# A second cycle of both MLPs computed by Strassen's scheme, in a two-layer fp32 transformer step

## The chip, the cores and the metric

The kernel runs on one core of one Trainium2 chip. The metric is the device time in microseconds (us) of one execution, as the median of a few runs. The four compute engines are TensorE (PE, with its weight loads as PEld), VectorE (DVE), ScalarE (ACT) and GpSimd (POOL); SyncE (SP) issues nearly all DMAs. They run side by side and meet at semaphores.

## The reference, cut to what matters

The reference is one step of a hybrid backbone with two layers on 640 tokens (512 latent, 128 context) of width 1024. Layer 0 mixes by a convolution module and a retention scan, layer 1 by grouped-query attention. The change touches only the MLP that ends each layer:

```python
h = rmsnorm(x, norm_g[layer, 1]) * (1 + sc2) + sh2
x = x + g2 * (jnp.square(jax.nn.relu(h @ mlp_w1[layer])) @ mlp_w2[layer])
```

with `mlp_w1` of 1024x4096 and `mlp_w2` of 4096x1024. The scales, shifts and gates (`sc2`, `sh2`, `g2`) come from the conditioning vector times `ada_w`, a product that in layer 0 is computed in small pieces between the matmuls of the MLP, for what follows it.

## The kernel before

**Number format.** Each fp32 operand is split into a high part (what fp32r keeps, a copy by ScalarE) and a low part (operand minus high part, by VectorE or GpSimd). A product is three matmuls: high by high, high by low, low by high. Names end in H and L (`hH`, `hL`; `wH`, `wL`; `fH`, `fL`). Tokens stand in the free dimension as two halves of 320 columns, so that nearly each matmul is 128x128 weights by 320 columns.

**The MLP by cycles.** `CYCLES` = 8 cycles of 512 hidden columns run one behind the other. A cycle has a first product (h times 1024x512 of `mlp_w1`), relu and square, and a second product (the square times 512x1024 of `mlp_w2`) that is added into `xT`. The first `PLAIN` = 2 cycles are plain: 8 x 4 x 2 x 3 = 192 matmuls for each product, 384 a cycle. Cycles 2 to 6 (the set `W2`) use one level of Strassen's scheme (Winograd's form) in both products: seven half-size products instead of eight, so 7 x 24 = 168 matmuls for each, 336 a cycle. The last cycle has the first product by Strassen and the second plain.

**What a Strassen product needs.** The weights' seven operands are B11, B22, B21, read from HBM, and four sums, T1 = B12 - B11, T3 = B22 - B12, T2 = T3 + B11, T4 = B21 - T2 (`add_blocks`; the keys are "p" for the first product, "q" for the second). VectorE makes the sums, ScalarE the high parts (`split_product`), and the low parts are made by VectorE for T2, T3, T1, B22, B21, T4 of "p" (`P_DVE`, made by `t_lo`) and by GpSimd for B11 of "p" and all of "q" (`lo`, L2033). High and low parts lie in a ring of four buffers (`wH`, `wL`), the raw blocks in another ring of four, and SyncE loads a block when the buffer's last reader has signalled (`wait_raw_free`). The tokens' side of the first product needs A11, A12, A22, which are views of h, and four sums S1 to S4 of blocks of h. These are the same in all cycles, so they are made once a layer (`add_s` L2511, `s_split` L1830, `s_low` L2525), before the change in cycles 0 and 1. The high and low part of S1 take the place of the block of h in `hH` and `hL` that only plain cycles read.

**Order inside a first Strassen product.** TensorE goes B11, T2, T3, T1, B22, B21, T4, two groups (m = 0, 1) of 12 matmuls each. B11, T2, T3, T4 accumulate in banks 6 and 7; between them ScalarE copies the partial sums out (`partials` L1764: `p1` after B11, `u2` after T2, `u3` after T3), and T2's first group waits for `p1`. B22's groups accumulate on T1's banks once VectorE has taken T1's sum out (`combine` L2582), which waits in VectorE's program order behind two weight sums, "p" T4 and "q" T3. "q" T3 needs the raw block "q" B22 from HBM. At the end of a Strassen cycle ScalarE splits B11, T2, T3 and T1 of the next one, in this order, and only then turns to `p1`; VectorE makes the sums T3, T2, T1, the low parts of T2 and T3 and the updates `product_out` (L2617, L2620, L2622) in a written order.

**Layer 0 alone** also has three short products with `ada_w` in each cycle (`strips`, L866; in a Strassen cycle the first stands between B11 and T2, the second between T1 and B22, the third between T4 and T1 of the second product), the 1 MB loads of `ada_w` for them in SyncE's queue between the weight blocks, and `modulate` on VectorE.

**The plain cycle.** ScalarE takes the relu out of the bank (L1758), VectorE squares it (L2500), ScalarE and VectorE split the square; then 16 groups of the second product run through four banks, each bank free when VectorE's `residual` (L2069) of the group four places before is done. VectorE's further work (`s_steps`, `p_add`, `t_lo`) is written out by group number (`after`).

Of the kernel before, what the change touches and what calls it, by code (L numbers as in the profile page):

```python
# [26 lines left out]
P = 128  # L27
# [4 lines left out]
HALF = T // 2  # L32
# [13 lines left out]
CYCLES = FF // 512  # L46
PLAIN = 2
# [40 lines left out]
P_DVE, SUM_ORDER = (T2, T3, T1, B22, B21, T4), (T3, T2, T1, T4)  # L88
# [56 lines left out]
F_CYCLE = {0: 0, 1: 8, CYCLES - 1: 16}  # L145
F_LAYER = 24
# [106 lines left out]
def hybrid_step(nc, x_prompt, x_sample, state_ret, cache_k, cache_v, ada_w, even_w_in, even_w_out, final_g,  # L253
# [3 lines left out]
    with ctx:  # L257
# [3 lines left out]
        def place(name, shape, dt=F32):  # L261
# [77 lines left out]
        s4_raw = nc.alloc_sbuf_tensor_at("s4_raw", [P, 4, HALF], F32, offset=here[0] + 24 * HALF)  # L339
# [5 lines left out]
        s1_raw = nc.alloc_sbuf_tensor_at("s1_raw", [P, 4, HALF], F32, offset=here[0])  # L345
# [392 lines left out]
        def _(pe):  # L738
# [436 lines left out]
            def first_strassen(layer, c, v, part):  # L1175
# [13 lines left out]
                pe.wait_ge(s_ready, 4 * layer + 4)  # L1189
# [262 lines left out]
        def _(act):  # L1452
# [291 lines left out]
            def mlp_layer(layer):  # L1744
# [102 lines left out]
                for c in range(CYCLES):  # L1847
                    t, g, s = t0 + 4 * c, g0 + G_CYCLE[c], WINO * layer + c - PLAIN
                    if 0 < c < PLAIN:
# [5 lines left out]
                        s_split(2, 5)  # L1855
                        s_split(3, 6)
                        s_split(4, 8)
                    elif c:
                        partials(c, p1, 1, p1_done)
                        split_product("p", s, B22, g + 2)  # L1860
                        partials(c, u2, 3, u2_done)
                        split_product("p", s, B21, g + 4)
                        partials(c, u3, 5, u3_done)
                        split_product("p", s, T4, g + 6)
                    if c in W2:
# [19 lines left out]
                        for n, i in enumerate((B11, T2, T3, T1)):  # L1885
                            split_product("p", s + 1, i, g + 30 + 4 * n)
# [173 lines left out]
        def _(dve):  # L2060
# [71 lines left out]
            def h_both(norm, later):  # L2132
# [10 lines left out]
                h_lo(norm, 0, KC - 1)  # L2143
                reciprocal_std(norm, 1)
# [333 lines left out]
            def mlp_layer(layer, norm):  # L2478
# [37 lines left out]
                r2, r3, r4 = (s_raw[i][:] for i in (2, 3, 4))  # L2516
                s_steps = [lambda: add_s(r3, *h_block(0, 1), ALU.add), lambda: add_s(r2, *h_block(4, 1), ALU.add),
                           lambda: add_s(s1_raw[:], r3, r2, ALU.add, 2), lambda: add_s(r4, *h_block(0, 0), ALU.add),
                           lambda: add_s(r2, s1_raw[:], r4, ALU.subtract, 4), lambda: add_s(r3, r4, r3, ALU.subtract, 4),
                           lambda: add_s(r4, *h_block(4, 0), ALU.add, 6), lambda: add_s(r4, r4, r2, ALU.subtract, 7)]  # L2520
# [112 lines left out]
                def strassen_cycle(c):  # L2633

                    s, s2 = WINO * layer + c - PLAIN, len(W2) * layer + c - PLAIN
                    t_lo(s, T1)
                    modulate(c, 0)
# [48 lines left out]
                    t_lo(s + 1, T2)  # L2686
# [3 lines left out]
                    t_lo(s + 1, T3)  # L2690
# [38 lines left out]
                for c in range(CYCLES):  # L2729
                    if c == 0:  # L2730
                        hidden(0, {5: [lambda: weight_lo(t0 + 2)]})
                    elif c < PLAIN:
                        hidden(c, {2: [lambda: modulate(c, 0)], 3: s_steps[4:5], 4: s_steps[5:6], 5: s_steps[6:7],
                                   6: s_steps[7:8]})
# [6 lines left out]
                    if c == 0:  # L2741
                        modulate(0, 1)
                    after = {8: [lambda: modulate(c, 2)]} if c % 2 == 0 else {10: [lambda: modulate(c, 2)]}
                    if c == 0:
                        after.update({2 + 2 * n: after.get(2 + 2 * n, []) + [step] for n, step in enumerate(s_steps[:4])})
                    if c == PLAIN - 1:
                        for n, i in ((8, T3), (9, T2), (11, T1)):
                            after[n] = after.get(n, []) + [lambda i=i: p_add(WINO * layer, i)]
                        for n, i in ((12, T2), (14, T3)):
                            after[n] = after.get(n, []) + [lambda i=i: t_lo(WINO * layer, i)]  # L2750
                        after[1] = [lambda: s_low(2, 1)]
                        after[3] = [lambda: s_low(3, 2)]
                        after[4] = [lambda: s_low(4, 3)]
                        after[5] = [lambda: s_low(1, 4)]
# [216 lines left out]
```

## Time and profile before

| | us |
|---|---|
| median of 3 runs | 1544.29 (1543.58 to 1544.55) |
| the profiled execution's own time | 1546.61 |
| its span, first to last instruction | 1544.8 |
| PE busy in it | 1513.4 (98%) |
| DVE busy | 1157.0 (75%) |
| ACT busy | 682.6 (44%) |
| POOL busy | 550.1 (36%) |
| mean granted TensorE clock | 0.996 of full speed |

Shares are of the span. A matmul's record is longer than the spacing of matmuls, because they are pipelined; so the time of many matmuls is read from starts, or from a stretch. The MLP of layer 0 runs from about 415 to 863 us, that of layer 1 from about 1108 to 1530 us; cycle 1 of them starts at 478.1 and 1166.7.

### The profile page before, as it was taken

How to read it: one execution, taken by the hardware profiler on the slowest of the kernel's cores; microseconds unless marked ns; L12 is line 12 of the kernel's file. 1: busy time of each engine (PE TensorE's matmuls, PEld its weight loads, DVE VectorE, ACT ScalarE, POOL GpSimd, SP SyncE). 2: the span in 40 equal slices, each digit the busy share in tenths (PEclk: the TensorE clock that was granted, in tenths of full speed). 3: DMA queues.
4: the chain of work that ended last, by engine and by line, in shares of the span. 5: the costliest groups of instructions: out<-in, count | busy, mean ns of one | idle time of the engine just before them, and what ended most of it. 6: DMA issues, size and time to landing. Idle time of an engine off the chain costs nothing. (4 is left out here: it accounts for less than half of the span.)

```text
span 1544.8 us, 28343 instructions
## 1 busy us (share of the span) xinstructions
PE 1513.4 (98%) x11754; PEld 1476.9 (96%) x11754; DVE 1157.0 (75%) x1901; ACT 682.6 (44%) x1140; POOL 550.1 (36%) x362
## 2 busy tenths in 40 slices
PE   8999999999999999999999999999999999999998
PEld 7999999999999999999999999999999999999998
DVE  5348678675684878898897888773584798899886
ACT  5323333334442354455455534652442355545553
POOL 0233313314323343563454253101333265446531
PEclk9999999999999999999999999999999999999999
DMA  9455334213233334433435121001222222322222
GB/s 327 154 177 168 102 101 154 83 53 125 76 123 109 124 118 165 134 135 132 137 131 169 35 83 62 28 1 55 83 69 69 69 69 81 98 82 69 83 83 83
DMA packets 123168, 162.20 MB, mean 105 GB/s; under 512 B 4640, under 2 KB 87584, under 8 KB 123040
## 3 DMA queue, kind: packets, MB, share of 16 engines
q1 hardware_dynamic: 121808, 159.34, 32.0%
q8 instruction: 93, 1.52, 0.4%
q10 hardware_dynamic: 1232, 1.05, 0.2%
q14 instruction: 35, 0.29, 0.1%
HBM read 156.44 MB, written 3.93 MB: 104 GB/s over the span
## 5 line engine op out<-in xcount | busy, mean ns | idle before, releaser
L2033 POOL TENSOR_TENSOR wL<-raw,wH 128x512 fp32r<-128x512 f32 x188 | 304.8, 1648 | 793.6 <-ACT wH L1463 532.0
L1171 PE MATMUL ps<-fx,wH 128*128 128x320 f32 x1120 | 248.0, 310 | 1.6 <-DVE held L2622 1.1
L747 PE MATMUL ps<-hH,wH 128*128 128x320 f32 x704 | 221.1, 314 | 1.9 <-DVE hL L2119 1.3
L747 PE MATMUL ps<-hH,wL 128*128 128x320 f32 x704 | 217.6, 309 | 0.0
L747 PE MATMUL ps<-hL,wH 128*128 128x320 f32 x704 | 217.5, 309 | 0.0
L1171 PEld LDWEIGHTS ps<-fx,wH 128*128 128x128 f32 x1120 | 186.8, 188 | 4.6 <-issue 4.0
L2033 POOL TENSOR_TENSOR wL<-raw_high,wH 128x512 fp32r<-128x512 f32 x100 | 141.1, 1438 | 128.2 <-ACT wH L1463 114.1
L1171 PE MATMUL ps<-fx,wL 128*128 128x320 f32 x560 | 173.0, 309 | 0.0
L747 PE MATMUL ps<-wH,hH 128*128 128x256 f32 x560 | 162.1, 290 | 2.4 <-POOL wL L2033 1.1
L747 PE MATMUL ps<-wL,hH 128*128 128x256 f32 x560 | 158.3, 283 | 0.0
L747 PE MATMUL ps<-wH,hL 128*128 128x256 f32 x560 | 158.3, 283 | 0.0
L2069 DVE SCALAR_TENSOR_TENSOR xT<-ps,modT,xT 128x192 f32<-128x192 f32 (+1 forms) x216 | 86.1, 433 | 79.5 <-PE ps L747 78.7
L747 PEld LDWEIGHTS ps<-hH,wH 128*128 128x128 f32 x704 | 132.2, 188 | 6.4 <-DVE hL L2119 2.8
L1171 PE MATMUL ps<-s,wH 128*128 128x320 f32 x576 | 128.9, 312 | 7.8 <-ACT p L1764 6.3
L747 PEld LDWEIGHTS ps<-hL,wH 128*128 128x128 f32 x704 | 132.2, 188 | 0.2
L747 PEld LDWEIGHTS ps<-hH,wL 128*128 128x128 f32 x704 | 132.2, 188 | 0.0
L747 PE MATMUL ps<-fH,wH 128*128 128x320 f32 x384 | 119.8, 312 | 0.2 <-DVE fL L2491 0.2
L1171 PE MATMUL ps<-hL,wH 128*128 128x320 f32 x384 | 118.7, 309 | 0.0
L1171 PE MATMUL ps<-hH,wL 128*128 128x320 f32 x384 | 118.6, 309 | 0.0
L1171 PE MATMUL ps<-hH,wH 128*128 128x320 f32 x384 | 118.6, 309 | 0.0
L747 PE MATMUL ps<-fL,wH 128*128 128x320 f32 x384 | 118.6, 309 | 0.0
L747 PE MATMUL ps<-fH,wL 128*128 128x320 f32 x384 | 118.6, 309 | 0.0
(303 smaller groups left out, 3753.7 us busy)
## 6 DMA issues: line engine op xcount, KB each, us to landing
ada<-in_ada_w SPq DMA_DIRECT2D x40, 1024.0 KB, 5.7
raw<-in_mlp_w SPq DMA_DIRECT2D x64, 512.0 KB, 3.8
raw_high<-in_mlp_w SPq DMA_DIRECT2D x64, 512.0 KB, 3.8
raw<-in_even_w_in SPq DMA_DIRECT2D x28, 512.0 KB, 5.8
pre_w<-in_ada_w SPq DMA_DIRECT2D x16, 512.0 KB, 8.9
raw<-in_odd_w_qkv SPq DMA_DIRECT2D x10, 512.0 KB, 3.6
raw<-in_even_w_out SPq DMA_DIRECT2D x8, 512.0 KB, 3.7
raw<-in_odd_w_o SPq DMA_DIRECT2D x6, 512.0 KB, 3.5
```

The lines of the kernel that those rows point to most:

```text
L747: last = nc.tensor.matmul(ps[:, bank, 0:width], a_, b_, start=(k == 0 and p_ == 0), stop=(k == nk - 1 and p_ == 2))
L1171: last = nc.tensor.matmul(ps[:, bank, 0:HALF], a_, b_, start=(opens and k == 0 and p_ == 0), stop=(k == nk - 1 and p_ == 2), skip_group_ch ...
L2033: last = nc.gpsimd.tensor_tensor(wL[:, at % 4, cs], source(key)[:, cs], wH[:, at % 4, cs].bitcast(F32), ALU.subtract)
L2069: last = nc.vector.scalar_tensor_tensor(out=x, in0=ps[:, n % 4, c0 - half * HALF:c0 - half * HALF + w_], scalar=modT[:, gate_at + k, which ...
```

## The change

`PLAIN` becomes 1, so that cycle 1 of both layers is a Strassen cycle and `W2` is 1 to 6. What was spread over cycles 0 and 1 for the first Strassen cycle now stands in cycle 0. The order of the sums of h changes, the first (of `hH` + `hL`, block 0, half 0) goes into the norm ahead of the MLP, behind the low parts of half 0 (`h_both`), one into the squares (`hidden`), and the others between the updates of the second product. The low part of S4 and that of T1 come at the start of cycle 1. The raw sums get other buffers: S2's over the end of `fq` and `p1`, S3's over `u2` and `u3`, S1's and S4's over the norm buffers and `held`, the first T3 over `fr`. TensorE, and ScalarE's partials, wait for each S by itself and not for all four.

`P_DVE` now differs by layer: in layer 0 the low parts of T2 and T3 of "p" are GpSimd's, in layer 1 VectorE's as before. And in layer 1, ScalarE's split of T1 moves from the end of the cycle before to behind `p1` in the cycle that uses it.

```diff
-PLAIN = 2
+PLAIN = 1
-P_DVE, SUM_ORDER = (T2, T3, T1, B22, B21, T4), (T3, T2, T1, T4)
+SUM_ORDER = (T3, T2, T1, T4)
+P_DVE = ((T1, B22, B21, T4), (T2, T3, T1, B22, B21, T4))
...
+        t3_begin = nc.alloc_sbuf_tensor_at("t3_begin", [P, 1024], F32, offset=here[0])
+        s2_raw = nc.alloc_sbuf_tensor_at("s2_raw", [P, 4, HALF], F32, offset=here[0] + 24 * HALF)
...
                 wait_low(pe, "p", s, T2)
-                pe.wait_ge(s_ready, 4 * layer + 4)
+                pe.wait_ge(s_ready, 4 * layer + 1)
...
                 wait_low(pe, "p", s, T3)
+                pe.wait_ge(s_ready, 4 * layer + 2)
...
                     if out is p1 and c == PLAIN:
-                        act.wait_ge(s_ready, 4 * layer + 4)
+                        act.wait_ge(s_sum, 8 * layer + 8)
+                        act.wait_ge(s_ready, 4 * layer + 1)
+                    elif out is u2 and c == PLAIN:
+                        act.wait_ge(s_ready, 4 * layer + 2)
...
                         partials(c, p1, 1, p1_done)
+                        if layer:
+                            split_product("p", s, T1, g)
                         split_product("p", s, B22, g + 2)
...
-                        for n, i in enumerate((B11, T2, T3, T1)):
+                        for n, i in enumerate((B11, T2, T3) if layer else (B11, T2, T3, T1)):
                             split_product("p", s + 1, i, g + 30 + 4 * n)
...
                     for q in range(4):
+                        if q == 1:
+                            s_split(4, 8)
...
+                        elif q < 3 or layer == 0:
                             split_product("p", s + 1, (B11, T2, T3, T1)[q], g + 8 + 4 * (q + 1))
-                        if c == PLAIN - 1 and q == 0:
+                        if q == 0:
                             act.wait_ge(acc_full, g + 8)
-                            s_split(1, 3)
+                            s_split(1, 4)
+                            s_split(3, 5)
+                            s_split(2, 6)
...
                 h_lo(norm, 0, KC - 1)
+                if norm in (1, 3):
+                    dve.wait_ge(h_ready, 16 * norm + 8)
+                    nc.vector.tensor_tensor(s_raw[2][:], hH[:, 0:4, 0:HALF].bitcast(F32), hL[:, 0:4, 0:HALF].bitcast(F32),
+                                            ALU.add).then_inc(s_sum, 1)
                 reciprocal_std(norm, 1)
...
                     t_lo(s, T1)
+                    if c == PLAIN:
+                        s_low(4, 4)
                     modulate(c, 0)
                     t_lo(s, B22)
...
-                    t_lo(s + 1, T2)
+                    if layer:
+                        t_lo(s + 1, T2)
...
-                    t_lo(s + 1, T3)
+                    if layer:
+                        t_lo(s + 1, T3)
...
+                        hidden(0, {5: [lambda: weight_lo(t0 + 2)], 6: s_steps[0:1]})
...
+                    after = {0: s_steps[1:2], 2: s_steps[2:3], 3: s_steps[3:4], 5: s_steps[4:5], 6: s_steps[5:6],
+                             8: [lambda: modulate(0, 2)] + s_steps[6:7], 9: [lambda: s_low(2, 3)],
+                             10: [lambda: p_add(p0, T3)], 11: [lambda: p_add(p0, T2)], 12: [lambda: s_low(3, 2)],
+                             13: [lambda: p_add(p0, T1)], 14: [lambda: t_lo(p0, T2)] if layer else [],
+                             15: ([lambda: t_lo(p0, T3)] if layer else []) + [lambda: s_low(1, 1)]}
```

## Rows read from the trace of the kernel before

**Rows 1.** The page: busy us of an engine, its share of the span, instructions.
```profile
PE 1513.4 (98%) x11754; PEld 1476.9 (96%) x11754; DVE 1157.0 (75%) x1901; ACT 682.6 (44%) x1140; POOL 550.1 (36%) x362
```
**Rows 2.** Waits of PE, whole span: us in total, times, longest.
```profile
PE ps L1171 <- ACT p L1764: 6.3, 5, 1.3
```
**Rows 3.** Stretches, by the cycles of both MLPs: length, busy us of each engine, granted clock.
```profile
478.10:538.20 60.10, 60.10 (x482) 58.69 (x481) 39.39 (x57) 19.07 (x28) 20.53 (x12) 1.00 0.33 106
538.20:591.20 53.00, 53.00 (x434) 51.81 (x433) 42.09 (x59) 25.98 (x35) 23.64 (x16) 1.00 0.39 130
591.20:645.90 54.70, 53.34 (x434) 51.73 (x433) 46.29 (x64) 26.95 (x36) 26.75 (x16) 1.00 0.41 136
645.90:699.40 53.50, 53.12 (x434) 51.72 (x433) 47.79 (x61) 26.99 (x36) 25.20 (x16) 1.00 0.40 138
...
1166.70:1223.30 56.60, 56.60 (x386) 56.36 (x385) 38.62 (x53) 19.06 (x28) 20.56 (x12) 1.00 0.19 57
1223.30:1273.00 49.70, 49.60 (x339) 49.36 (x338) 41.77 (x54) 25.04 (x34) 26.86 (x16) 1.00 0.25 75
1273.00:1324.10 51.10, 49.72 (x338) 49.25 (x337) 46.32 (x60) 26.64 (x36) 26.83 (x16) 1.00 0.27 83
```
**Rows 4.** Timeline of PE, start of layer 1's cycle 3: start, us, instruction [idle before].
```profile
1276.18 0.31 PE L1171 MATMUL ps<-hL,wH 128*128 128x320 f32 x1
1276.32 0.31 PE L1171 MATMUL ps<-hH,wL 128*128 128x320 f32 x1
1277.91 0.53 PE L1171 MATMUL ps<-s,wH 128*128 128x320 f32 x2 [1.28 <-ACT p L1764]
```
**Rows 5.** Timeline of ACT, the same place.
```profile
1276.38 1.06 ACT L1481 ACTIVATE wH<-raw 128x1024 fp32r<-128x1024 f32 x1 [1.54 <-DVE raw L2566]
1277.35 0.75 ACT L1764 ACTIVATE p<-ps 128x320 f32<-128x320 f32 x2
```
**Rows 6.** Timeline of DVE, the same cycle.
```profile
1279.67 1.22 DVE L2531 TENSOR_TENSOR wL<-raw_high,wH 128x1024 fp32r<-128x1024 f32 x1
1285.74 1.23 DVE L2566 TENSOR_TENSOR t_first<-raw_high,raw 128x1024 f32<-128x1024 f32 x1
```
**Rows 7.** Load of "q" B22 in that cycle: first and last issue; then time to landing.
```profile
L541 SPq DMA_DIRECT2D raw_high<-in_mlp_w x1: 367/367/367, 1280.9 to 1280.9; - x1
...
DMA to landing us min/median/max: 4.5/4.5/4.5
```
**Rows 8.** Timeline of DVE, layer 0's cycle 3.
```profile
607.14 1.23 DVE L2566 TENSOR_TENSOR t_first<-raw_high,raw 128x1024 f32<-128x1024 f32 x1 [3.58 <-DMA raw_high<-in_mlp_w]
608.29 0.48 DVE L2582 TENSOR_TENSOR fq<-ps,u 128x320 f32<-128x320 f32 x1
```
**Rows 9.** Timeline of PE, layer 0's cycle 3.
```profile
608.92 0.53 PE L1171 MATMUL ps<-s,wH 128*128 128x320 f32 x2 [1.24 <-DVE fq L2582]
```
**Rows 10.** Timeline of DVE, layer 1, norm and cycle 0.
```profile
1117.05 2.16 DVE L2098 RECIPROCAL ps<-rstd 128x320 f32<-128x320 f32 x1 [2.59 <-ACT rstd L1494]
...
1144.68 2.33 DVE L2511 TENSOR_TENSOR s_raw<-hH,hL 128x1280 f32<-128x1280 f32 x1
1146.93 1.20 DVE L2069 SCALAR_TENSOR_TENSOR xT<-ps,modT,xT 128x192 f32<-128x192 f32 x3
...
1151.69 1.48 DVE L2511 TENSOR_TENSOR s_raw<-s_raw 128x1280 f32<-128x1280 f32 x1
```
**Rows 11.** Timeline of POOL, the low parts: two instructions make one block.
```profile
581.31 2.56 POOL L2033 TENSOR_TENSOR wL<-raw_high,wH 128x512 fp32r<-128x512 f32 x2 [0.71 <-ACT wH L1481]
...
607.84 3.89 POOL L2033 TENSOR_TENSOR wL<-raw,wH 128x512 fp32r<-128x512 f32 x2 [20.87 <-ACT wH L1481]
```
**Rows 12.** Timeline of POOL: the slowest pair of layer 1.
```profile
1203.52 5.04 POOL L2033 TENSOR_TENSOR wL<-raw,wH 128x512 fp32r<-128x512 f32 x2
```
**Rows 13.** Timeline of ACT, end of layer 0's cycle 2.
```profile
590.08 1.06 ACT L1481 ACTIVATE wH<-t_first 128x1024 fp32r<-128x1024 f32 x1 [7.26 <-DVE t_first L2566]
591.04 1.05 ACT L1481 ACTIVATE wH<-t_second 128x1024 fp32r<-128x1024 f32 x1
```

More of the change, by code:

```diff
@@ L120, with T_LOW_AT @@
     raw_last_[buf_] = key_
+def T_LOW_AT(s, i):
+    layer, n = divmod(s, WINO)
+    return layer * WINO * len(P_DVE[0]) + n * len(P_DVE[layer]) + P_DVE[layer].index(i) + 1
 BLOCK_AT = {key: n for n, key in enumerate(BLOCKS)}
-POOL_LO = [key for key in BLOCKS if key[0] == "q" or (key[2] not in P_DVE if key[0] == "p" else key[0] not in DVE_LO)]
+POOL_LO = [key for key in BLOCKS if key[0] == "q" or (key[2] not in P_DVE[key[1] // WINO] if key[0] == "p" else key[0] not in DVE_LO)]
 POOL_AT = {key: n + 1 for n, key in enumerate(POOL_LO)}
@@ L144 @@
 A_MLP1 = A_QKV + 30
-F_CYCLE = {0: 0, 1: 8, CYCLES - 1: 16}
-F_LAYER = 24
+F_CYCLE = {0: 0, CYCLES - 1: 8 * PLAIN}
+F_LAYER = 8 * PLAIN + 8
 def F_AT(c, half, k):
@@ L338, in hybrid_step @@
         fs = nc.alloc_sbuf_tensor_at("fs", [P, 2, HALF], F32, offset=here[0] + 16 * HALF)
-        s4_raw = nc.alloc_sbuf_tensor_at("s4_raw", [P, 4, HALF], F32, offset=here[0] + 24 * HALF)
+        t3_begin = nc.alloc_sbuf_tensor_at("t3_begin", [P, 1024], F32, offset=here[0])
+        s2_raw = nc.alloc_sbuf_tensor_at("s2_raw", [P, 4, HALF], F32, offset=here[0] + 24 * HALF)
         fq = place("fq", [P, 4, 2, HALF])
@@ L344, in hybrid_step @@
         p1 = place("p1", [P, 2, HALF])
-        s1_raw = nc.alloc_sbuf_tensor_at("s1_raw", [P, 4, HALF], F32, offset=here[0])
+        s3_raw = nc.alloc_sbuf_tensor_at("s3_raw", [P, 4, HALF], F32, offset=here[0])
         u2 = place("u2", [P, 2, HALF])
@@ L350, in hybrid_step @@
         t24_first = place("t24_first", [P, 1024])
-        s2_raw, s3_raw = (nc.alloc_sbuf_tensor_at(f"s{n}_raw", [P, 4, HALF], F32, offset=norm_buffers + 16 * HALF * j)
-                          for j, n in enumerate((2, 3)))
+        s1_raw, s4_raw = (nc.alloc_sbuf_tensor_at(f"s{n}_raw", [P, 4, HALF], F32, offset=norm_buffers + 16 * HALF * j)
+                          for j, n in enumerate((1, 4)))
         s_raw = {1: s1_raw, 2: s2_raw, 3: s3_raw, 4: s4_raw}
-        t3_begin = nc.alloc_sbuf_tensor_at("t3_begin", [P, 1024], F32, offset=norm_buffers)
         held = nc.alloc_sbuf_tensor_at("held", [P, KC, HALF], F32, offset=norm_buffers)
@@ L504, in wait_low @@
         def wait_low(engine, *key):
-            if key[0] == "p" and key[2] in P_DVE:
-                engine.wait_ge(t_low, len(P_DVE) * key[1] + P_DVE.index(key[2]) + 1)
+            if key[0] == "p" and key[2] in P_DVE[key[1] // WINO]:
+                engine.wait_ge(t_low, T_LOW_AT(*key[1:]))
             elif key in FIRST_BLOCKS:
@@ L1197, in first_strassen @@
                 wait_low(pe, "p", s, T1)
+                pe.wait_ge(s_ready, 4 * layer + 3)
                 pe.wait_ge(dve_free, v)
@@ L1202, in first_strassen @@
                 wait_low(pe, "p", s, B22)
+                pe.wait_ge(s_ready, 4 * layer + 4)
                 for m in range(2):
@@ L2514, in h_block @@
                     return [x[:, k0:k0 + 4, halfcols(half)].bitcast(F32) for x in (hH, hL)]
[L2516 to L2520, printed above, removed]
+                r1, r2, r3, r4 = (s_raw[i][:] for i in (1, 2, 3, 4))
+                s_steps = [lambda: add_s(r4, *h_block(0, 1), ALU.add), lambda: add_s(r1, *h_block(4, 1), ALU.add),
+                           lambda: add_s(r1, r4, r1, ALU.add, 3), lambda: add_s(r3, r2, r4, ALU.subtract, 3),
+                           lambda: add_s(r2, r1, r2, ALU.subtract, 5), lambda: add_s(r4, *h_block(4, 0), ALU.add, 5),
+                           lambda: add_s(r4, r4, r2, ALU.subtract, 7)]
                 def s_low(i, count):
@@ L2730, in mlp_layer @@
                     if c == 0:
[L2731 to L2734, printed above, removed]
+                        hidden(0, {5: [lambda: weight_lo(t0 + 2)], 6: s_steps[0:1]})
                     elif c in W2:
@@ L2740, in mlp_layer @@
                         break
[L2741 to L2754, printed above, removed]
+                    modulate(0, 1)
+                    p0 = WINO * layer
+                    after = {0: s_steps[1:2], 2: s_steps[2:3], 3: s_steps[3:4], 5: s_steps[4:5], 6: s_steps[5:6],
[3 more added lines that the diff above has]
+                             15: ([lambda: t_lo(p0, T3)] if layer else []) + [lambda: s_low(1, 1)]}
                     for n in range(16):
```

4 lines of the change are left out of this document (removed).

## The prediction, made before the changed kernel was run

> **What bounds the kernel now.** I read the page's busy times first [rows 1]: TensorE is busy 98% of the span, no other engine over 75%. So what counts is how many matmuls there are, and the little time that TensorE waits. Second, TensorE's waits [rows 2]: the largest group by far is five waits for ScalarE's copy `p1`, 6.3 us together. Third, the stretches cut at the cycles [rows 3]. The granted clock is 1.00 in all of them. A plain cycle takes 60.1 us in layer 0 and 56.6 in layer 1; the first Strassen cycle 53.0 and 49.7; a later one 54.7 or 53.5 and 51.1. The ratio 56.6 / 384 gives 0.147 us a matmul, and 336 of them make 49.4, so the first Strassen cycle of layer 1 has almost no idle time. Layer 0's 53.0 holds 3.6 more for three short products, 1.2 each. Two things are to be seen: the later cycles are 0.5 to 1.7 us longer than the first, and in them VectorE is busy 46 to 48 us of 51 to 54, near a bound of its own.
>
> Fourth, the timelines at the place of a wait. In layer 1 the last matmul of B11 starts at 1276.32 and the first of T2 at 1277.91 where 1276.47 was due [rows 4]: 1.44 us lost. ScalarE shows why [rows 5]: it could have copied `p1` soon after 1276.4, but its split of T1 stands ahead, and that began only at 1276.38, when VectorE had made the sum. The wait comes in cycles 3 to 7, five times. Layer 0 hides it behind its short product. There another wait shows: at 607.14 VectorE has sat idle 3.58 us for a block from HBM [rows 8], and TensorE starts B22 at 608.92, 1.24 idle [rows 9], 0.63 behind the start of the combination at 608.29.
>
> **The change part by part.** The sum is made on the profiled execution, 1546.6 us, of which 1544.8 is the span; the median of the runs is 1544.3, 2.3 less, and the saving is carried over to it.
>
> *Matmuls.* Each converted cycle loses 48, so 96 x 0.147 = 14.1 us go. By the stretches: cycle 1 falls from 56.6 to 49.7 in layer 1 and from 60.1 to 53.0 in layer 0 if the new first Strassen cycle is as clean as the old one. That is -6.9 and -7.1; the short products stay three.
>
> *T1 split behind `p1`, layer 1.* `p1` is then ready with B11's end. Behind it the split of T1 ends about 1278.3, before VectorE comes to T1's low part at 1278.5 (it ends where the next row begins, 1279.67 [rows 6]), so nothing there moves. `u2` waits behind the splits of T1 and B22 (1.06 each) and is ready some 0.3 before T3 wants it. So 1.44 goes, five times, and one later cycle more exists. What is late next: the load of "q" B22 is issued when VectorE has done B22's low part, 1280.9, and takes 4.5 [rows 7]. It lands at 1285.4, just ahead of the sum at 1285.74 [rows 6]. This does not move, while TensorE comes 1.44 earlier. The sum then ends at 1286.6, B22 can start 0.63 behind that, 1287.3; due are six groups behind T2, 1276.47 + 72 x 0.147 = 1287.1. So 0.2 comes back, and a later cycle of layer 1 takes 51.1 - 1.44 + 0.2 = 49.9. Bounds: 49.5 (nothing back) to 51.1 (all back). I take the lower part, since each step has a row.
>
> *Norm.* The new sum of h (1.4 to 1.5 us) stands where VectorE idles 2.59 us for the standard deviation [rows 10]; in both layers, so nothing.
>
> *Cycle 0.* VectorE had room; now it makes all sums of h and three weight sums there. From the first update, at 1143.2 in layer 1: 16 updates at 0.46 (half 0) and 0.66 (half 1, two instructions; three instructions took 1.2 [rows 10]) are 9.0; six sums of h at 1.45 are 8.7, three low parts of them 4.3, three weight sums 3.4, low parts of T2 and T3 2.3; together 27.7. A sum that met GpSimd took 2.33 and not 1.48 [rows 10], and GpSimd has four instructions in the first part; I add 2. VectorE is through at about 1173, 6 us into cycle 1, and its updates stay ahead of the banks by 0.5 to 3 us, except near group 8 where I put 0.3 us of waiting (bounds 0 and 1.5). T2's low part comes at 1169.6, due 1170.3: in time. But T1's and S4's low parts follow (1.15 + 1.4), then B22's at 1176.6, 9.9 us into the cycle. The load of "q" B22 starts there, 3.8 us at that quiet time (the 4.5 of rows 7 overlaps another), the sum takes 1.2, B22 can start at +15.5, due 96 x 0.147 = +14.1: about 1.3 us of waiting. Bounds: 0 (VectorE's own slack is taken) and 3.
>
> *Layer 0, cycle 1.* The same with one `modulate` more, GpSimd working on T2 and T3 against VectorE's last low parts, and a 1 MB load in the queue ahead of "q" B22. I come to B22's low part at +11, landing at +16.4, B22 at +18.2, due +14.1 and two short products, +16.5: 1.7 to 2, taken as 2.0 (bounds 0 and 4; the nearest row, cycle 3, lost 1.7 in the same wait).
>
> *T2 and T3 low parts to GpSimd, layer 0.* Their high parts are ready at 591.1 and 592.1 [rows 13]; GpSimd is idle from 587 to 607.8 [rows 11] and takes 2.56 for a block, 3.9 when it meets VectorE. T2 is due at 591.2 + 3.5 + 1.2 = 595.9 and comes at 593.7 to 595.0; T3 due 599.4, comes at 596.3 to 598.9. So it is hidden, with 0.5 us to spare at the worst. VectorE loses 2.3 us of work just where it is late: T1's and B22's low parts come 1 us earlier, hence the load behind the 3.58 us gap [rows 8] too. I give cycle 3 a gain of 1.0, cycles 4 to 6 of 0.25 each, and cycle 2, now a later one, costs 0.2. Bounds for the part: a gain of 3.2 (all that cycles 3 to 6 have over 53.0 [rows 3]) and a loss of 3.
> The Trainium skill (SBUF — State Buffer, "Who interferes with whom") says that a VectorE instruction with two SBUF inputs and a GpSimd instruction reading SBUF exclude each other for a whole instruction, whoever starts first. The trace agrees with its 2.33 against 1.48; by it four more GpSimd instructions could hold VectorE up to four times a cycle, which would eat the gain and bring this part to about 0.
>
> *Sum.* Layer 0: cycle 1 -60.1 + 53.0 + 2.0 = -5.1; cycle 2 +0.2; cycle 3 -1.0; cycles 4 to 6 -0.75: -6.65. Layer 1: cycle 0 +0.3; cycle 1 -56.6 + 49.7 + 1.3 = -5.6; cycle 2, 49.7 to 49.9, +0.2; cycles 3 to 6 and the first product of 7, -1.2 each, -6.0: -11.1. Together -17.8: 1546.6 - 17.8 = 1528.8 for a profiled execution, and a median of 1526.5.
>
> **The rivals.**
> *B, the gain of the moved split is given back.* For it: VectorE has only some 4.8 us idle in a later cycle of layer 1 (46.3 of 51.1 [rows 3]), and the load's time does not move. Against: its idle time lies before the place where it becomes late. If all five waits return (+6.2), or the first Strassen cycles wait 3 us more each, the time is 1532.7.
> *C, all is hidden.* No waits in cycle 1 of either layer (-3.3), none in cycle 0 and none returned (-1.5), layer 0's later cycles at 53.0 (-1.7): 1520.0. Against it: the load of "q" B22 hangs on a late VectorE in both layers.
> *D, GpSimd is late for T3 (slower than before).* In layer 0 the two blocks of low parts come in each of cycles 1 to 7. If their four instructions go at the slowest pair's pace (5.04 for a block [rows 12]) and each block waits once more for a VectorE instruction, T3 is ready at 591.1 + 10.1 + 2.3 = 603.5, 4.1 us late; 7 x 4.1 = 29 us, so 1555. It decides against the change from 2.5 us a cycle on (17.8 / 7). Against it: the pace of rows 11, and GpSimd's 20 us of idle time at that place.
> *E, the low parts are on the path once each.* GpSimd takes 2.56 where VectorE takes 1.22 for the same block; 14 blocks x 1.35 = 19 us, all of it on the path, gives 1545.5, no change.
> The Trainium skill (GPSIMD Engine Reference, "Engine selection") says to put elementwise work on VectorE because GpSimd is about twice as slow with two inputs; this is E. The trace agrees with the ratio (2.56 to 1.22), but shows slack ahead of T2 and T3.
>
> **How the numbers follow.** Forecast 0.57, with its own range 1522.5 to 1530.5; B 0.20; C 0.15; E 0.04; D 0.04. A change under 0.2% (3.1 us) can't be told from none here; only E falls within it and only D is slower, so faster 0.92, same 0.04, slower 0.04. The range goes from below C to above B, 1519 to 1534, and leaves out E, D and the ends of B and C, near 0.15.
>
> **What would show it.** Right: 96 matmul records fewer; the group "PE ps <- ACT p" gone from TensorE's waits; later cycles of layer 1 near 49.9 with a small wait for `fq` at B22; cycle 1 near 51.0 and 55.0 with its wait at B22 behind the HBM block; GpSimd busy some 3 us more in each cycle of layer 0. Wrong: a wait of TensorE for `wL` of GpSimd at T2 or T3 (D, E); later cycles of layer 1 near 51 with the wait at B22, or at T2 of the second product (B); cycle 0 longer than 0.5 us more.

## The result

| | median us | runs | range us | ratio to before, 95% |
|---|---|---|---|---|
| before | 1544.25 | 4 | 1543.58 to 1544.55 | |
| changed | 1531.28 | 4 | 1529.75 to 1531.53 | 0.9911 [0.9899, 0.9923] |

The change takes 13.0 us away. The forecast was 1526.5 (range 1519 to 1534, own range of the likeliest case 1522.5 to 1530.5): the sign and the range held, the saving is 13.0 instead of 17.8, and the number lies nearer to rival B's 1532.7. The profiled execution of the changed kernel took 1531.19 us with a span of 1529.3.

The page after, line by line beside [rows 1]: 96 matmuls fewer, VectorE busy 51.6 us more (the sums and low parts of a second converted cycle in each layer), GpSimd 53.9 more.

```profile
PE 1499.2 (98%) x11658; PEld 1462.3 (96%) x11658; DVE 1208.6 (79%) x1925; ACT 708.8 (46%) x1162; POOL 604.0 (39%) x390
```

TensorE's waits in the whole span, beside [rows 2]: three groups of the changed kernel (us in total, times, longest). The group for ScalarE's `p`, 6.3 us, is gone. What has grown is VectorE's `fq` (B22 of the first product), 1.2 us before, `held` (T2 of the second product), 1.1 before, and the last low parts `fL` of cycle 0's squares, 0.2 before.

```profile
PE ps L1180 <- DVE fq L2604: 2.9, 5, 0.8
PE ps L1180 <- DVE held L2644: 2.8, 7, 0.6
PE ps L756 <- DVE fL L2513: 2.6, 3, 1.0
```

The stretches by cycles, beside [rows 3]: layer 0's cycles 0, 1, 3 and 6, then layer 1's 0 to 3.

```profile
414.37:478.14 63.77, 61.88 (x484) 59.18 (x483) 60.34 (x102) 29.11 (x54) 20.64 (x15) 1.00 0.36 116
478.14:531.13 52.99, 52.99 (x435) 51.74 (x433) 47.99 (x65) 26.41 (x35) 33.01 (x20) 1.00 0.42 140
584.06:637.02 52.96, 52.96 (x434) 51.76 (x433) 44.31 (x62) 26.68 (x36) 31.68 (x20) 1.00 0.41 140
743.50:798.31 54.81, 53.47 (x435) 51.75 (x433) 47.42 (x61) 27.06 (x36) 33.14 (x20) 1.00 0.40 135
1088.86:1160.41 71.55, 69.60 (x467) 68.33 (x465) 66.11 (x115) 34.25 (x61) 20.94 (x14) 1.00 0.20 60
1160.41:1210.88 50.47, 49.77 (x339) 49.31 (x337) 47.03 (x58) 24.92 (x34) 27.20 (x16) 1.00 0.28 84
1210.88:1261.15 50.27, 49.76 (x338) 49.29 (x337) 46.98 (x60) 26.77 (x36) 27.25 (x16) 1.00 0.28 84
1261.15:1311.43 50.28, 49.67 (x339) 49.29 (x337) 47.19 (x60) 26.77 (x36) 27.43 (x16) 1.00 0.28 85
```

Cut in the same way in the kernel before, layer 0's cycle 0 took 62.63 and layer 1's 69.71. The converted cycle 1 is as short as hoped or shorter (52.99, 50.47). Layer 1's later cycles are 50.3, where 49.9 was forecast. Layer 1's cycle 4 is the exception, 50.58. And both cycles 0 are longer, by 1.14 and 1.84 us, where 0 and 0.3 were forecast.

### The profile page after: what moved, and what is told of

The parts are those of the page before. It is cut to its first block and busy times, and to the rows that moved or that the text cites. A ratio compares the mean times of both kernels' runs of the same rounds, so it can differ in the third digit from the quotient of the medians.

```text
span 1529.3 us, 28267 instructions
## 1 busy us (share of the span) xinstructions
PE 1499.2 (98%) x11658; PEld 1462.3 (96%) x11658; DVE 1208.6 (79%) x1925; ACT 708.8 (46%) x1162; POOL 604.0 (39%) x390
## 5 line engine op out<-in xcount | busy, mean ns | idle before, releaser
L1180 PE MATMUL ps<-fx,wH 128*128 128x320 f32 x1344 | 297.5, 310 | 3.0 <-DVE held L2644 2.8
L1180 PEld LDWEIGHTS ps<-fx,wH 128*128 128x128 f32 x1344 | 224.1, 188 | 6.2 <-issue 5.9
L1180 PE MATMUL ps<-fx,wL 128*128 128x320 f32 x672 | 207.6, 309 | 0.0
L1180 PEld LDWEIGHTS ps<-fx,wL 128*128 128x128 f32 x672 | 126.2, 188 | 0.0
L2051 POOL TENSOR_TENSOR wL<-t_second,wH 128x512 fp32r<-128x512 f32 x60 | 101.7, 1716 | 52.9 <-ACT wH L1493 52.7
L1180 PEld LDWEIGHTS ps<-s,wH 128*128 128x128 f32 x672 | 111.5, 188 | 7.8 <-issue 6.0
L756 PEld LDWEIGHTS ps<-hH,wH 128*128 128x128 f32 x576 | 108.2, 188 | 6.0 <-DVE hL L2137 2.8
L756 PEld LDWEIGHTS ps<-wH,hH 128*128 128x128 f32 x560 | 107.2, 191 | 3.6 <-DVE xT L2087 1.4
L2087 DVE SCALAR_TENSOR_TENSOR xT<-ps,modT,xT 128x320 f32<-128x320 f32 (+2 forms) x168 | 66.8, 432 | 55.4 <-PE ps L756 55.1
L756 PEld LDWEIGHTS ps<-hL,wH 128*128 128x128 f32 x576 | 108.2, 188 | 0.2
```

The costliest lines, as they stand in the source:

```text
L756: last = nc.tensor.matmul(ps[:, bank, 0:width], a_, b_, start=(k == 0 and p_ == 0), stop=(k == nk - 1 and p_ == 2))
L1180: last = nc.tensor.matmul(ps[:, bank, 0:HALF], a_, b_, start=(opens and k == 0 and p_ == 0), stop=(k == nk - 1 and p_ == 2), skip_group_ch ...
L2051: last = nc.gpsimd.tensor_tensor(wL[:, at % 4, cs], source(key)[:, cs], wH[:, at % 4, cs].bitcast(F32), ALU.subtract)
L2087: last = nc.vector.scalar_tensor_tensor(out=x, in0=ps[:, n % 4, c0 - half * HALF:c0 - half * HALF + w_], scalar=modT[:, gate_at + k, which ...
```

## Where the two terms went wrong, in the trace

*Cycle 0.* VectorE, GpSimd and TensorE in layer 1, where the square's last two groups are made (start, us, instruction, idle before):

```profile
1130.97 1.49 DVE L2533 TENSOR_TENSOR s_raw<-hH,hL 128x1280 f32<-128x1280 f32 x1
1132.37 1.59 DVE L2522 TENSOR_TENSOR fs<-fr 128x320 f32<-128x320 f32 x1
1133.88 3.04 DVE L2513 TENSOR_TENSOR fL<-fs,fH 128x320 fp32r<-128x320 f32 x2
```
```profile
1132.19 5.88 POOL L2051 TENSOR_TENSOR wL<-raw_high,wH 128x512 fp32r<-128x512 f32 x4 [25.24 <-ACT wH L1475]
```
```profile
1136.98 0.41 PE L756 MATMUL ps<-fH,wH 128*128 128x320 f32 x1 [0.78 <-DVE fL L2513]
```

The sum of h moved into the squares (1130.97) pushes the square of group 7 to 1132.37, just behind GpSimd's first low part. From there the two engines alternate: each of three VectorE instructions of 0.49 us takes 1.5 to 1.6, the length of a GpSimd instruction. TensorE's third group of the second product waits twice, 1.79 us together, in layer 1 and once, 0.78, in layer 0.

The kernel before had a little of this. In its layer 1 only the last low part met GpSimd, behind a wait for ScalarE's copy, which stood behind the split of a weight tile; TensorE waited 0.22:

```profile
1141.62 1.64 DVE L2491 TENSOR_TENSOR fL<-fs,fH 128x320 fp32r<-128x320 f32 x1 [1.41 <-ACT fH L1752]
```

*Later cycles of layer 1.* VectorE's chain in cycle 3, from the first sum of the second product's weights to the first product group:

```profile
1273.53 1.23 DVE L2588 TENSOR_TENSOR t_first<-raw_high,raw 128x1024 f32<-128x1024 f32 x1 [1.25 <-DMA raw_high<-in_mlp_w]
1274.68 0.49 DVE L2604 TENSOR_TENSOR fq<-ps,u 128x320 f32<-128x320 f32 x1
...
1276.61 2.33 DVE L2553 TENSOR_TENSOR wL<-raw_high,wH 128x1024 fp32r<-128x1024 f32 x1
1278.87 0.48 DVE L2604 TENSOR_TENSOR fq<-ps,u 128x320 f32<-128x320 f32 x1
1279.27 1.92 DVE L2588 TENSOR_TENSOR raw<-raw 128x1024 f32<-128x1024 f32 x1
1281.11 0.48 DVE L2604 TENSOR_TENSOR fq<-ps,u 128x320 f32<-128x320 f32 x1
1281.51 1.52 DVE L2630 TENSOR_TENSOR fx<-fq,fx 128x640 fp32r<-128x640 f32 x1
...
1286.64 2.31 DVE L2588 TENSOR_TENSOR t_second<-raw_high,t_second 128x1024 f32<-128x1024 f32 x1
1288.87 0.81 DVE L2630 TENSOR_TENSOR fx<-u,fx 128x640 fp32r<-128x640 f32 x1
1289.61 0.88 DVE L2644 TENSOR_TENSOR held<-ps,held 128x320 f32<-128x320 f32 x2
```
```profile
1290.23 0.39 PE L1180 MATMUL ps<-fx,wH 128*128 128x320 f32 x1 [0.61 <-DVE held L2644]
```

It runs 16.6 us with 0.65 us of idle time. Four of its instructions take longer than usual beside GpSimd (2.33, 2.31 and 1.92 where 1.22 is usual, 1.52 where 0.81 is usual), which works from 1276.57 to 1287.87: 3.6 us. In the kernel before VectorE had caught up with TensorE once on this way, in the second of the two `fq<-ps,p`,

```profile
1295.79 0.49 DVE L2582 TENSOR_TENSOR fq<-ps,p 128x320 f32<-128x320 f32 x1 [0.94 <-PE ps L1171]
```

since TensorE had lost 1.44 us at `p1`. Now it does not. The last matmul ahead of T2 starts at 1289.32, so T2 was due 0.147 later, at 1289.47, and came 0.76 late; with 0.16 late at B22 that is all of the 0.9 us that a later cycle (50.28) takes over its 336 matmuls at 0.147 (49.4). The prediction had 0.2 returned at B22 and left the old 0.35 at T2 as it was, without looking there.

## The experiments

All are edits of the changed kernel. Differences are those of the medians, against the 1531.38 us of its second run; the intervals in brackets are for the ratio to the kernel before and are 4 to 5 us wide, so a difference under 2 us rests on the stretches of the traces, one trace each. Both kernels were traced a second time: the changed kernel unchanged,

> The changed kernel unchanged, a second profile and five more rounds, as the base for its neighbours. Theory S (the sum of h that stands among the squares of cycle 0 makes the lateness there): cycle 0 again 63.8 us in layer 0 and 71.5 in layer 1, with TensorE idle 0.8 and 1.8 us in the third group of the second product. Rival N (that was an accident of one execution): cycle 0 back near 62.6 and 69.7. Time 1530 to 1532 either way.

gave 1531.38 us (1530.97 to 1532.93), ratio 0.9916 [0.9901, 0.9931], a span of 1529.1 and the same cycles 0 to the hundredth, 63.77 and 71.55. So theory S's lateness is no accident. One thing was: layer 0's cycle 6, 54.81 in the first trace, is 53.51 here. The kernel before:

> The kernel before once more, for a second trace: its first profiled execution lay 2.3 us above its median. If that was an accident of one stage, one stretch is some 1 us longer in the first trace than in this one and the span is near 1542.5; if the profile adds it, the span is 1544.8 again.

It took 1543.64 with a span of 1541.8. Of the 3.0 us between the two spans, 0.85 lie in layer 0's cycles 5 and 6, 0.3 ahead of cycle 1, and 1.75 in its cycle 3, 54.72 in the first trace [rows 3, 8, 9] and here

```profile
583.84:636.81 52.97, 52.97 (x434) 51.73 (x433) 46.84 (x61) 27.01 (x35) 26.49 (x17) 1.00 0.42 144
```

So the 1.24 us wait of [rows 9], from which the prediction took a gain, was an accident of that execution. What differs is the load of "q" B22: it landed 8.4 us after its issue in the long cycle 3 and 6.2 in this one, and 8.1 in the 54.81 us of the changed kernel's cycle 6 against 6.9 in its 53.51. Each time the 1 MB load issued just ahead of it was late as well (8.3 and 6.0, 8.7 and 7.5). Why the loads took longer is not shown.

**Cycle 0.** Three edits.

```
# e_sum_n5:    hidden(0, {5: [weight_lo(t0 + 2), s_steps[0]]})      (was 6: s_steps[0:1])
# e_act_order: hidden_hi(0, 7); split(t0 + 3, g0 + 8)               (was the other way round)
# e_sum_after: hidden(0, {5: [weight_lo(t0 + 2)]}); after = {0: s_steps[0:1], 1: s_steps[1:2], ...
```

> The first sum of h in cycle 0 goes ahead of the square of group 6 instead of behind it; the same instructions, the same count. There VectorE idles 1.68 us (layer 0) and 0.48 us (layer 1) for ScalarE. Theory S (the short squares come one behind the other, each held by a GpSimd instruction of 1.5 us): the square of group 7 starts 1.5 and 0.5 us earlier, one of the three held instructions gets ahead of GpSimd's block, cycle 0 loses 1 us in layer 0 and 1.5 in layer 1, total -2.5 us. Rival V (VectorE's work in cycles 0 and 1 together is the bound, wherever it stands): cycle 0 shorter by as much, but B22 of cycle 1 waits 1.5 us more in layer 1; total -1. Rival N: no change.

Measured 1529.72 (1529.19 to 1530.42), 0.9904 [0.9889, 0.9919], 1.7 us less than the changed kernel. In the traces cycle 0 is 62.64 in layer 0 (-1.13) and 1.03 shorter in layer 1: theory S, where -1 and -1.5 were expected. Only one `fL` is held now. Cycle 1 of layer 1 is 50.77, and 50.47 and 50.55 in the two traces of the changed kernel: V takes back 0.3 us at most.

> ScalarE copies the high part of the last square of cycle 0 before it splits the next weight tile, instead of behind it; nothing else changes. GpSimd's four low parts of that tile can start only behind the split, so they no longer meet the last two low parts of the squares. Theory S with contention as its cause: the two instructions that took 1.56 us take 0.49, TensorE's third group of the second product waits 0.5 us or less, cycle 0 is 1.0 us shorter in layer 0 and 1.8 in layer 1, the total falls by 1.5 to 2.8 us. If the sum's own 1.49 us is the cause and not the contention: at most 0.5 us in each layer, total -0.5 to -1. Rival V: gained in cycle 0, given back in cycle 1 of layer 1; total -1.

Measured 1528.31 (1526.95 to 1529.25), 0.9894 [0.9877, 0.991], 3.1 us less. The same place in layer 1, VectorE and then GpSimd:

```profile
1129.49 1.49 DVE L2533 TENSOR_TENSOR s_raw<-hH,hL 128x1280 f32<-128x1280 f32 x1
1130.89 0.49 DVE L2522 TENSOR_TENSOR fs<-fr 128x320 f32<-128x320 f32 x1
1131.29 1.12 DVE L2513 TENSOR_TENSOR fL<-fs,fH 128x320 fp32r<-128x320 f32 x2
```
```profile
1132.91 10.05 POOL L2051 TENSOR_TENSOR wL<-raw_high,wH 128x512 fp32r<-128x512 f32 x4 [27.43 <-ACT wH L1475]
```
```profile
1087.38:1156.61 69.23, 69.08 (x467) 68.32 (x465) 63.64 (x115) 34.25 (x61) 25.20 (x14) 1.00 0.20 62
```

The sum of h stands where it stood and takes as long; the three short instructions behind it take 0.49 each (the two `fL` together 1.12, with a short pause), and TensorE's wait at this place is gone. Cycle 0 is 2.32 us shorter in layer 1, 1.13 in layer 0. That is the contention, and not the sum's own 1.49 us. The swap also lets ScalarE's copy come earlier, but in the changed kernel VectorE had no idle time for that copy (rows above), and ScalarE itself stood idle for 0.93 us until VectorE had made the square. By an estimate from these rows (ScalarE's split over at 1133.06, a copy of 0.47, then 0.49), both `fL` would have been done at about 1134.0 without the contention, and TensorE wanted the first at 1134.33. The contention does not vanish: GpSimd's four instructions take 10.05 now instead of 5.88, but nobody waits for them. In layer 1 the cycle is also 0.48 shorter than in the kernel before (69.23 to 69.71), so part of these 3.1 us is the old lateness of the last `fL` and no loss of the change. Cycle 1 of layer 1 is 50.69, so V takes back 0.2 at most.

> The first sum of h leaves the squares of cycle 0 and stands behind its first update, the next one behind the second. Theory S: the squares of cycle 0 go as in the kernel before, cycle 0 is 62.6 and 69.7 us, -1.1 and -1.8. But all later work of VectorE in the cycle stands where it did while TensorE comes 1.8 us earlier. Rival V (VectorE's chain sets cycle 1 of layer 1): T2's low part of cycle 1 ends at the same time as before, due 1.8 us earlier, and B22 waits 2.3 instead of 0.5; the total is within 0.5 us of the changed kernel in layer 1 and -1.1 in layer 0: -1.1. Without V the total is -2.9.

Measured 1530.88 (1529.93 to 1532.08), 0.9912 [0.9897, 0.9926], 0.5 less, which the intervals don't tell from nothing. In the trace cycle 0 is 63.14 in layer 0 and 0.6 shorter in layer 1, 1.25 us in sum of the 2.9; in part of the rest's stead TensorE waits, here in layer 1:

```profile
PE ps L756 <- DVE xT L2087: 0.7, 2, 0.3
PE ps L756 <- DVE fL L2513: 0.2, 1, 0.2
```

Cycle 1 did not become longer (50.52), so V, whose total was nearer, had the place wrong: what is lost is lost within cycle 0, most of it at the updates. S is right about the cause, wrong in that the sum could simply be put elsewhere.

**The parts undone.**

```
# e_split_back: layer 1: split_product("p", s + 1, T1, ...) again at the end of the cycle before
# e_low_dve:    P_DVE = (T2, T3, T1, B22, B21, T4) for both layers, t_lo of T2, T3 in both
```

> One part undone: in layer 1 ScalarE splits T1 again at the end of the cycle before, ahead of its copies p1. Theory P (the prediction's step: the wait for p1 is worth 1.44 us a cycle, less what returns at B22): the group of TensorE's waits for ScalarE's p comes back, later cycles of layer 1 go from 50.3 to 51.1, cycle 1 stays at 50.5 (its T1 is split late anyway) or gains as well; total +0.8 x 5 to +1.3 x 6, so 1535.5 to 1539. Rival G (the wait is only exchanged for the one at B22 and for VectorE's later lateness): total +1.5 or less.

Measured 1535.57 (1534.99 to 1536.97), 0.9944 [0.9932, 0.9957]: +4.2 us, theory P, at the lower end. Over the whole span, and a later cycle:

```profile
PE ps L1180 <- ACT p L1776: 7.5, 6, 1.2
```
```profile
1213.34:1264.50 51.16, 49.76 (x338) 49.30 (x337) 46.39 (x60) 26.66 (x35) 26.92 (x16) 1.00 0.27 83
```

The wait of [rows 2] is back, six times, and a later cycle takes 51.15, as before. So the split is worth 51.15 - 50.3 = 0.85 us a cycle, not 1.2.

> One part undone: T2's and T3's low parts are VectorE's in layer 0 as well, and GpSimd has 14 blocks less. Theory M (VectorE's load is what made layer 0's later cycles long): cycle 3 back from 53.0 to 54.7, the others within 0.3 of 52.9 to 53.5, cycle 1 from 53.0 to 54.5 with a wait at B22; total +2 to +4 us, 1533.5 to 1535.5. Rival R (it makes no difference in layer 0, which has slack by its short products): within 0.7 us of 1531.4.

Measured 1534.0 (1532.23 to 1535.61), 0.9933 [0.992, 0.9945]: +2.6 us, within M's numbers. But the trace has little of M: layer 0's cycle 1 is 53.20 (not 54.5), cycle 2 53.51 (+0.6), cycle 3 52.99 (not 54.7), cycle 4 0.6 shorter; a cycle 6 of 54.78 and 1 us in layer 1's cycle 4 have appeared in other kernels too. Cycle 6's is a late load of "q" B22 again (8.1 us). I read 0.3 to 0.8 us for the part itself from the stretches; whether the rest of the median's 2.6 is chance or the part's own stays open.

**The later cycles of layer 1.**

```
# e_pool_t3:  P_DVE[1] without T3; GpSimd makes T3's low part in layer 1
# e_t4_after: layer 1: q_add(s2, T4) behind the first four product_out instead of ahead of operand_lo(S2_)
# e_fill_gap: e_act_order, and in layer 1  combine(c, F11, 0); t_lo(s, T4); q_add(T3); combine(c, F11, 1); q_add(T2)
#             (was q_add(T3); combine(c, F11, 0); q_add(T2); combine(c, F11, 1); t_lo(s, T4))
```

> One step further: in layer 1 T3's low part (not T2's) goes to GpSimd. Theory L (a later cycle of layer 1 waits 0.5 us at B22 since VectorE's row of low parts T3, T1, B22 frees B22's buffer late and the load behind it lands at 1324.45 with 1324.5 the sum's start): VectorE is through with B22's low part 0.4 to 0.6 us earlier (the splits of ScalarE come 0.6 ahead of VectorE now), the wait goes nearly, later cycles 49.8, total -2 to -3. Rival X (what VectorE gains in its own work it loses to GpSimd's instructions in the same stretch, each of which holds one of its own): total between -0.7 and +2.

Measured 1533.65 (1532.07 to 1534.48), 0.993 [0.9916, 0.9944]: +2.3, beyond both ranges. Later cycles stay at 50.3, so theory L is out and the rows are rival X's; what X does not hold is the rest, for 1.5 of the 1.6 us that this trace's span is longer lie in layer 1's cycle 0 and have another cause, shown behind the next run. Why VectorE was not earlier, in cycle 3 (VectorE, then GpSimd):

```profile
1263.07 1.22 DVE L2553 TENSOR_TENSOR wL<-t_first,wH 128x1024 fp32r<-128x1024 f32 x1
1264.21 2.31 DVE L2588 TENSOR_TENSOR raw<-raw 128x1024 f32<-128x1024 f32 x1
```
```profile
1264.06 3.62 POOL L2051 TENSOR_TENSOR wL<-t_second,wH 128x512 fp32r<-128x512 f32 x2 [5.20 <-ACT wH L1493]
```

The 1.22 us taken off VectorE come back as 1.1 us on the sum that meets GpSimd. B22's load is issued 7.98 us into the cycle, against 7.94 in the changed kernel.

> Measures the disputed cost: in layer 1 the load of the second product's block B22 brings only half of its rows (0.26 of 0.52 MB), so this kernel leaves out the new values of the other half. Theory L: the load lands 1 us or more earlier, the sum q T3 starts at once behind VectorE's work, the wait for fq at B22 goes in all six cycles (0.5 to 0.8 each) and cycles come to 49.7 to 49.8; total -3 to -3.5. What is left over 49.5 is the wait for held at T2 of the second product. Rival W (VectorE's own chain ends no earlier than the load): -1 or less.

This one did not test what it was meant to. The block has only two chunks of rows, the edit took both, and the issue's row still says

```profile
raw_high<-in_mlp_w SPq DMA_DIRECT2D x1, 512.0 KB, 4.5
```

It is the changed kernel once more, nothing left out: 1531.23 (1529.29 to 1534.27), 0.9917 [0.9903, 0.993]. As a third trace it shows what varies: layer 1's cycle 4 takes 50.58, 51.03 and 51.91 us in the three, with the load of "q" B22 landing 5.1, 5.5 and 6.4 us after its issue, where the other cycles have 3.9 to 4.8. And cycle 0 of layer 1 took 1.5 us more in the third. There the granted clock of TensorE fell to its lower level, 1.2 GHz, for 3.4 us, right behind the two waits for `fL`:

```profile
1138.00:1141.00 3.00, 3.00 (x13) 3.00 (x13) 3.00 (x5) 0.40 (x1) 0.00 (x0) 0.50 0.61 181
```

Matmuls start 0.267 us apart in it instead of 0.147. The same fall, at 1137.1, makes the 1.5 us of e_pool_t3's cycle 0. Away from the start and the end of the kernel it stands in these two traces alone, while the two waits ahead of it stand in both traces of the changed kernel too; so no run shows what brings it about. Whether a shorter load would help was not tried.

> In layer 1 VectorE makes the sum T4 of the second product's weights behind the first four product groups instead of between the sum S2 and its low part; it took 2.31 us there, held by GpSimd. Theory Q (what a later cycle of layer 1 has over its 336 matmuls, 0.95 us in three profiles whatever stood before it, is VectorE's chain from the combination of F22 to the first product group, and the waits at B22 and at T2 only share it): the wait for held at T2 goes, T2's operand is ready 1.5 us earlier, later cycles come to 49.7 with only the 0.2 to 0.35 at B22 left, total -0.6 x 6 = -3.5 us, 1527.5 to 1528.5. Rival Z (T4's split, its low part on GpSimd and the operands behind it come late instead): TensorE waits for GpSimd's wL or for fx at T4, cycles 50.3 or longer, total from 0 to +3.

Measured 1535.56 (1534.01 to 1539.06), 0.9948 [0.9934, 0.9962]: +4.2, rival Z, at another tile than it named. TensorE's waits in the later cycles:

```profile
PE ps L1180 <- DVE xT L2639: 4.7, 5, 1.0
PE ps L1180 <- DVE fq L2604: 1.7, 5, 0.7
```

and GpSimd behind the moved sum:

```profile
1292.61 3.14 POOL L2051 TENSOR_TENSOR wL<-t_second,wH 128x512 fp32r<-128x512 f32 x2 [4.99 <-ACT wH L1493]
...
1298.80 3.73 POOL L2051 TENSOR_TENSOR wL<-raw_high,wH 128x512 fp32r<-128x512 f32 x2
```

The wait for `held` did go, as theory Q says. But GpSimd now idles 5 us until the moved sum is split, and then works without a pause beside VectorE's last operands; its updates come late, and a cycle takes 51.0.

> Both at once: ScalarE's last copy of cycle 0 ahead of its split, and the sum T4 behind the first product groups in layer 1. If the two are independent, -3.1 (measured for the first) and -3.5: 1524.8 us. If cycle 1 of layer 1 gives back what cycle 0 gains, 1526.5. If theory Q is wrong, 1528.

Measured 1532.82 (1532.19 to 1534.8), 0.9926 [0.9914, 0.9939]. None of the three numbers: cycle 0 gave its 3.5 us in the trace (1.15 and 2.34), the moved sum made the later cycles 50.7 to 51.7 again. The measured +1.4 is near the sum of the two single measurements (-3.1 and +4.2): they are independent, and one of them is a loss.

> ScalarE's last copy of cycle 0 ahead of its split (as in e_act_order, 1528.3 us), and in layer 1 VectorE does the first combination and T4's low part while it waits for the block B22 of the second product (idle there 1.25 us and more in each later cycle), then the sums T3 and T2. Theory Q (the chain of VectorE from that landing to the first product group sets the 0.95 us a later cycle loses): T4's low part no longer meets GpSimd's (2.33 to 1.22 us) and the chain ends 1.0 us earlier, the wait at T2 of 0.4 to 0.84 us goes and the one at B22 too, since its combination no longer stands behind the landing; later cycles 49.5 to 49.7, 1523 to 1525 us. Rival Z (the lateness turns up further down, as when the sum T4 was moved): cycles 50.3 to 51, a wait for another tile in the second product, 1528 to 1532.

Measured 1527.06 (1525.18 to 1528.38), 0.9885 [0.9869, 0.9902], the lowest ratio of all; from e_act_order's 0.9894 the intervals don't tell it; the 1.2 us between the two profiled spans (1525.0 and 1526.2) are the stretches of cycles 1 and 4 below. VectorE in cycle 3 of layer 1:

```profile
1267.05 1.22 DVE L2588 TENSOR_TENSOR raw_high<-raw_high,t_first 128x1024 f32<-128x1024 f32 x1
1269.65 0.49 DVE L2604 TENSOR_TENSOR fq<-ps,u 128x320 f32<-128x320 f32 x1 [1.38 <-PE ps L1180]
1270.06 1.22 DVE L2553 TENSOR_TENSOR wL<-raw_high,wH 128x1024 fp32r<-128x1024 f32 x1
1271.19 1.22 DVE L2588 TENSOR_TENSOR t_first<-raw_high,raw 128x1024 f32<-128x1024 f32 x1
1272.33 0.48 DVE L2604 TENSOR_TENSOR fq<-ps,u 128x320 f32<-128x320 f32 x1
1272.73 2.20 DVE L2588 TENSOR_TENSOR t_second<-t_first,raw 128x1024 f32<-128x1024 f32 x1
```
```profile
PE ps L1180 <- DVE held L2644: 3.8, 5, 0.8
```

Half of the expectation came. Every wait for `fq` is gone, cycle 1 takes 50.27 and cycle 4 50.27 (50.69 and 51.07 in e_act_order), since the combination no longer stands behind a load that may be late. But a regular later cycle is 50.3 once more, its 0.9 us now at T2 alone (the row above is for cycles 2 to 6 together). T4's low part is not held any more (1.22), but the sum T2 that took its place is: 2.20. And the combination, put first, makes the chain begin with TensorE's group: VectorE idles 1.38 us ahead of it, where T4's low part could have been done. That order, low part first, was not tried.

What the traces of the changed kernel, of e_act_order and of e_fill_gap have in common is that VectorE's chain begins near the end of T1's first group, be it by the landing or by that group, holds the same work and four meetings with GpSimd, and that the lateness comes to 0.9 us in sum. By that reading theory Q holds, and it was the place of the gap that I filled wrongly; the last step is argued from these rows, not shown by a kernel.

## Why the prediction was right, and where not

The second traces of both kernels (spans 1541.8 and 1529.1) differ by 12.7 us, as the medians do by 13.0; they are free of the accidents in layer 0's cycles 3 and 6. Against the working's terms:

| term | predicted | measured |
|---|---|---|
| layer 0, cycle 0 | 0 | +1.15 |
| layer 0, cycle 1 | -5.1 | -7.20 |
| layer 0, cycle 2 | +0.2 | 0.0 |
| layer 0, cycle 3 | -1.0 | 0.0 |
| layer 0, cycles 4 to 6 | -0.75 | +0.3 |
| layer 1, cycle 0 | +0.3 | +1.9 |
| layer 1, cycle 1 | -5.6 | -6.0 |
| layer 1, cycle 2 | +0.2 | +0.65 |
| layer 1, cycle 3 to the end | -6.0 | -3.15 |
| before the MLP | 0 | -0.3 |
| sum | -17.8 | -12.7 |

- *Matmuls*: 96 fewer, right, and cycle 1 in layer 0 as clean as the old first Strassen cycle, in layer 1 0.8 us longer.
- *Cycle 1*: the 2.0 us wait at B22 did not come in layer 0; of the 1.3 in layer 1 some 0.8 came. The estimate of VectorE's lateness after cycle 0 was too long; in layer 0 the bound 0 was the right end. These 2.5 us cover a third of what the other terms missed: without them the time would be 1533.8, at the edge of the range. That it lies well inside is in part luck.
- *T1's split behind `p1`*: the mechanism is right, shown by undoing it; the term was mis-sized, 0.85 us a cycle for 1.2, and cost the forecast the most (-3.15 us for -6.0). I had asked what is late next at B22 alone. The wait that grew most stands 15 us further on, at T2 of the second product.
- *Low parts of T2, T3 to GpSimd*: not on the path, no wait for GpSimd's `wL` in a Strassen cycle (D and E did not come). Its gain in cycle 3 was read from one execution's accident, and of the slack in cycles 5 and 6 the second trace of the kernel before has 0.85 us less. Undoing the part cost 2.6 us by the median and 0.3 to 0.8 by the stretches, so its worth is not settled.
- *Cycle 0*: the step that failed. "except near group 8 where I put 0.3 us of waiting": the updates did keep pace. What I left out was the last part of the squares. I had counted the sum's 1.49 us against VectorE's work as a whole and added 2 us for meetings with GpSimd, but had not looked where the sum stood: ahead of three short instructions on TensorE's path, beside GpSimd's four. It cost 3.0 us in two layers for 0.3.

The Trainium skill (SBUF — State Buffer, "Who interferes with whom") says that whichever of the two engines issues first blocks the other for its whole instruction, and that issue order decides who pays. The trace agrees with its rows at this place: 1.5 us a time on VectorE's side in the changed kernel, 10.05 instead of 5.88 on GpSimd's once the order is turned. In the prediction I gave the rule a price in layer 0's later cycles, where no such loss was seen, and here only as 2 us of VectorE's work, not as a wait of TensorE.

## What to carry to other kernels

An instruction's price is that of its place: before putting work into a queue, look which short instructions stand behind it on the path, and which other engine's block they will then meet. Where two engines hold each other up, let the one that nobody waits for start last; here two swapped lines on ScalarE gave 3.1 us. When a wait on a chain is taken away, follow that chain to its next meeting with the bounding engine, not only to the nearest one, and take no gain from a stretch that only one execution shows.

## What the hardware did that I had not expected

- An instruction of 0.49 us on VectorE took 1.56 to 1.59 us three times in a row beside GpSimd instructions of 1.5, as if the two took turns. A sum of 1.22 us that met GpSimd took 2.31 to 2.33, so a meeting cost some 1.1 us for either length: what counted here was how many instructions met, not how long they were.
- In the same stretch VectorE's updates that read PSUM were not held: three in 1.13 us at 1134.18 in e_act_order, in the midst of GpSimd's 10.05.

```profile
1132.79 1.48 DVE L2533 TENSOR_TENSOR s_raw<-hH,hL 128x1280 f32<-128x1280 f32 x1
1134.18 1.13 DVE L2087 SCALAR_TENSOR_TENSOR xT<-ps,modT,xT 128x320 f32<-128x320 f32 x3
```

- The same load lands later in one fixed cycle (layer 1's cycle 4) in every execution of the changed kernel that was traced, 5.1 to 6.4 us for 3.9 to 4.8 in the other cycles. No run here shows why.
- In two traces the granted clock fell to 1.2 GHz for 3.4 us in the midst of a busy kernel, behind waits of TensorE of 1.01 and 0.78 us, and cost 1.5 us.
